# Spreading the inverse roots of two norms over rows: a rounded part and the rest in place of one fp32 operand

## The chip, the cores and the metric

The kernel runs on one core of a Trainium2 chip. The metric is device time in microseconds (us) of one launch, as the median of several runs. TensorE (PE in the profile) does matrix products into PSUM, the accumulator memory (eight banks). VectorE (DVE), ScalarE (ACT) and GpSimd (POOL) work elementwise, and SyncE (SP) issues most of the transfers from DRAM. Every engine has a queue of its own that is worked off in order, and engines wait for one another by semaphores: an instruction that waits holds up all that stands behind it on its engine.

## The reference, cut to what matters

One step of a decoder trunk with two layers over 288 tokens (256 of a prompt and 8 x 4 samples), width 1024. A layer has four branches that read one input projection, gates, an output projection, and a SwiGLU block:

```
xn = rmsnorm(x, norm1_g);  z = xn @ w_in + b_in
o_gla = gla_recurrence(q, k, v, log_a, s0)                    # linear attention, 4 heads of 128
o_a = rmsnorm(o_gla, gla_norm_g) * silu(a_r)                  # norm over each head's 128 features
qd = rope(rmsnorm(d_q per head of 64, q_norm_g))              # 8 query heads
kd = rope(rmsnorm(d_k per head of 64, k_norm_g))              # 2 key heads
o_d = windowed_attention(qd, kd, vd)
x = x + (sum_b sigmoid(xn @ w_gate_b + b_gate_b) * (o_b @ w_branch_b)) @ w_out
x = x + (silu(g) * up) @ w_down,   g, up = rmsnorm(x, norm2_g) @ w_gate_up
```

rmsnorm(v) = v * rsqrt(mean(v*v) + 1e-6) * g. Two of these norms matter here: the one of the queries and keys (over 64 features of a head), and the one of the linear attention's output (over 128).

## The kernel before, in words

Features lie on the 128 partitions and the 288 tokens along the free axis. Each layer's weights stream through a ring of four slots as 158 blocks: 34 of the input projection (blocks 0 to 33), 32 of the gates (34 to 65), 16 of the branches, 8 of the output projection, 44 of the SwiGLU input and 24 of its output. A block of the first two stages holds eight 128x128 weight tiles. The weights and activations of these products are each split in two: a part rounded to fp32r (`w_hi`, `x_hi`) and the rest (`w_lo`, `x_lo`), and a tile costs three matmuls that each go over the 288 columns once (L438 hi x hi, L439 hi x lo, L443 lo x hi), so a block is 24 of them. ScalarE writes `w_hi` of block t+3 while TensorE is at about block t (`split`, L906); the subtraction that gives `w_lo` is GpSimd's in the first two stages, but for a few blocks (L1750), and VectorE's later (L1272). The next load of a slot (L338, on SP) waits for that subtraction. Results of the input projection go to banks 0 and 1 in turn, which ScalarE drains (L911, L917); a block can't start before its bank is drained of the block two before.

All small work of the branches is put between the blocks by the table `STEP`: on TensorE and ScalarE a step with number n runs once block n of the layer is through (a step with a lower number than the current block follows its predecessor at once). VectorE has its small work in a fixed order, with the taps of the convolution in between in runs of a given length (`CONV_RUNS`).

The query and key norm goes like this. ScalarE squares five tiles (four of queries, one of keys). TensorE sums them by head (`qk_sums`, step 14, L483, five fp32 matmuls of 128 rows and 32 columns) into rows of banks 2 and 3. ScalarE makes exp(-0.5 ln(.)) of them (`rstd`, Ln at L925, Exp at L928, one of each for 128 rows and one for 32 rows) and writes `r5`. TensorE spreads each root from its row to the 64 rows of its head (`qk_turned`, step 15, L489): five fp32 matmuls of 32 rows x 128 columns with a 0/1 matrix `of_head`, on row strips 0, 1, 2, 3 and 0 of the array, into banks 2 to 6. VectorE multiplies (L1402, L1404) and goes on with the rotary part (L1408 to L1411); TensorE needs the result at step 25 (`scores0`), and VectorE takes the scores up at L1415.

The linear attention's norm: TensorE sums squares at step 52 (L695, with the sum of another norm, L458, behind it), ScalarE makes Ln of both (L1078, L1079) and Exp of both (L1080 `gla_rs`, L1081), and TensorE spreads `gla_rs` at step 53, after gate block 19 (L704): four fp32 matmuls of 32 rows x 128 columns with the 0/1 matrix `spread`, one for each strip, into banks 2, 3, 6 and 7. VectorE waits for them and multiplies (L1539).

The constants lie in one tile `cst`. Its later part comes by one transfer that ScalarE issues at block 6 of layer 0 (L1175); TensorE first waits for it ahead of `lr_sums` (step 8, L475).

Of the kernel before, what the change touches and what calls it, by code (L numbers as in the profile page):

```python
# [27 lines left out]
P = 128  # L28
TS = DEC_B * DEC_T
# [55 lines left out]
PARAMS = _cols  # L85

CONST_AT, _cols = {}, 0
for _name, _n in (("ones", P), ("eps6", 1), ("eps5", 1), ("heads", TS), ("of_head", P), ("ident", P), ("upper", P), ("band", 2 * P),
                  ("new", 2 * (P + TS)), ("seg", T), ("cos", T), ("sin", T),
                  ("gla", 64), ("gla_s", TS), ("of_b", 4 * DEC_B), ("of_4", 2), ("rep", TS), ("spread", P)):  # L90
    CONST_AT[_name] = _cols
    _cols += _n
CONSTS = _cols

STEP = dict(
    chunk1=44, chunk2=45, chunk3=46, gla_spread=53, n1_sums=0, n1_rstd=0, n1_sums0=3, n1_rstd0=3, c_gate0=12,
    lr_sums=8, c_gate=8, qk_sq=14, qk_sums=14, qk_rstd=3, qk_turned=15, scores0=25, tok_copied=27, scores1=9,  # L100
    exp0=20, exp1=25, probs_turned=21, probs_copied=31, prompt_pv=26, prompt_od=25, smp_scores=27, conv0=35,
    conv1=48, exp_s=33, probs_s_turned=35, probs_s_copied=32, smp_pv=26, smp_od=36, decay_in=24, decay_log=22,
    v_copied=40, decay_exp=35, att_in=41, k_copied=43, gelu=46, chunks=43, smp_old=33, old_out=44, smp_out=47,
# [36 lines left out]
def trunk_program(nc, dram):  # L140
# [3 lines left out]
    with ctx:  # L144
        def sb(name, cols, dt=f32):
            return ctx.enter_context(nc.sbuf_tensor(name, [P, *cols], dt))
# [22 lines left out]
        x = sb("x", [KC, T])  # L169
        x_hi, x_lo = sb("x_hi", [KC, T], f32r), sb("x_lo", [KC, T], f32r)  # L170
        z, gate = zg[:, 0:NZ, :], zg[:, NZ:NZ + 4 * KC, :]
        work = sb("work", [6144])
        kv = sb("kv", [2048])
        prm = sb("prm", [PARAMS])
        cst = sb("cst", [CONSTS])
        w_lr = sb("w_lr", [KC, 32])
        w_a2 = sb("w_a2", [2 * P])
        w_sp = sb("w_sp", [4, P])
# [20 lines left out]
        def c(name, n=None, i=0):  # L199
            at = CONST_AT[name] + i  # L200
            return cst[:, at:at + (n or P)]


        added = work[:, 5760:5760 + T]
        sq = work[:, 0:KC * T].rearrange("p (c t) -> p c t", t=T)
        sq5 = work[:, 0:5 * T].rearrange("p (c t) -> p c t", t=T)
        r5 = work[:, 5 * T:10 * T].rearrange("p (c t) -> p c t", t=T)
        prob = work[:, 0:3072]
        prob_t = work[:, 3072:6144]
        prob0 = prob[:, 0:1024].rearrange("p (h k) -> p h k", k=P)  # L210
# [220 lines left out]
        def _(pe):  # L431
# [28 lines left out]
            def mixers(l, l1):  # L460
# [7 lines left out]
                sum_of(7, sq[:, 0, :], "n1_sums")  # L468
                yield from at("lr_sums")
                pe.wait_ge(E("w_lr_ready"), l1)  # L470
                pe.wait_ge(const_in, 16)
                pe.wait_ge(E("x_scaled"), l1)
                for k in range(KC):
                    part = slice(32 * (k % 4), 32 * (k % 4) + 32)
# [8 lines left out]
                    mm = pe.matmul(ps[r, 2 + k // 4, 0:T], c("heads", TS), sq5[:, k, :], start=True, stop=True)  # L483
                mm.then_inc(E("qk_sums"), 1)
                yield from at("qk_turned")
                pe.wait_ge(E("qk_rstd"), l1)
                for k in range(5):
                    r = slice(TS * (k % 4), TS * (k % 4) + TS)
                    mm = pe.matmul(ps[:, 2 + k, 0:T], c("of_head")[r], r5[r, k // 4, :], start=True, stop=True)  # L489
                mm.then_inc(E("qk_sums"), 1)  # L490
                yield from at("scores0")
                pe.wait_ge(E("qk_done"), l1)
# [205 lines left out]
                pe.wait_ge(E("cv_sq_added"), l1)  # L698
                sum_of(5, added, "cv_var")
                yield from at("gla_spread")  # L700
                pe.wait_ge(E("gla_rstd"), l1)
                for h in range(4):
                    r = slice(TS * h, TS * h + TS)
                    mm = pe.matmul(ps[:, GLA_BANKS[h], 0:T], c("spread")[r], gla_rs[r], start=True, stop=True)  # L704
                mm.then_inc(E("gla_spread"), 1)
                yield from at("smp_update0")
                pe.wait_ge(E("k_own_done"), l1)
# [181 lines left out]
        def _(act):  # L889
# [29 lines left out]
            def logs():  # L919
                act.preload_act_table_set("natural_log_exp_and_others")  # L920

            def rstd(l, out, sums, n, eps, event):

                for o, v in zip(out, sums):
                    ins = act.activation(o, v, ACT.Ln, scale=1.0 / n, bias=c(eps, 1)[0:o.shape[0]])  # L925
                link(ins, l)
                for o in out:
                    ins = act.activation(o, o, ACT.Exp, scale=-0.5)  # L928
                ins.then_inc(E(event), 1)
# [20 lines left out]
            def mixers(l, l1):  # L950
# [11 lines left out]
                    ins = act.activation(z[:, C_G + k, :], z[:, C_G + k, :], ACT.Sigmoid, bias=p("b_in", C_G + k))  # L962
                ins.then_inc(E("c_gate"), 1)
                yield from at("qk_sq")
                act.wait_ge(const_in, 16)
                act.wait_ge(E("lr_sums"), l1)
                act.wait_ge(xl_done, x_part_at(l, XN + KC - 1))
                for t in (D_V - 1, D_V):
# [2 lines left out]
                yield from at("qk_rstd")  # L971
                logs()
                act.wait_ge(E("qk_sums"), 2 * l + 1)
                rstd(l, [r5[:, 0, :], r5[0:TS, 1, :]], [ps[:, 2, 0:T], ps[0:TS, 3, 0:T]], HD, "eps6", "qk_rstd")
                yield from at("tok_copied")
                act.wait_ge(E("tok_turned"), l1)
                act.activation(vt[:, :, :].rearrange("p a n -> p (a n)"), ps[:, 6, 0:2 * P], ACT.Copy)
# [99 lines left out]

                act.activation(gla_rs, ps[:, 2, 0:T], ACT.Ln, scale=1.0 / P, bias=c("eps6", 1))  # L1078
                link(act.activation(rs_m[:, :], ps[:, 5, 0:T], ACT.Ln, scale=1.0 / 512, bias=c("eps5", 1)), l)  # L1079
                act.activation(gla_rs, gla_rs, ACT.Exp, scale=-0.5).then_inc(E("gla_rstd"), 1)  # L1080
                act.activation(rs_m[:, :], rs_m[:, :], ACT.Exp, scale=-0.5).then_inc(E("cv_rstd"), 1)  # L1081
                yield from at("r_silu")
# [81 lines left out]
            for l in range(DEPTH):  # L1164
# [3 lines left out]
                for t in range(NZ):  # L1168
                    if t > C_TILES:
                        drain_z(l, t - 1)  # L1170
                    if l == 0 and 2 <= t <= UNSCALED:
                        wait_block(act, l, Z0 + t - 1)
                        act.activation(z[:, t - 1, :], ps[:, (t - 1) % 2, 0:T], ACT.Copy).then_inc(bank_free[(t - 1) % 2], 1)
                    if l == 0 and t == CONSTS_AT:
                        act.dma_start(cst[:, FIRST_CONSTS:CONSTS], dram["consts"][:, FIRST_CONSTS:CONSTS]).then_inc(const_in, 16)  # L1175
                    split(g0 + t + 3)
                    if t == C_TILES - 1:
                        act.wait_ge(E("x_scaled"), l1)
                        for k in range(KC):
                            xn_part(l, k)  # L1180
                    place[0] = t
                    next(mix, None)
# [73 lines left out]
        def _(dve):  # L1256
# [139 lines left out]

            def mixers(l, l1, conv_steps):

                dve.wait_ge(const_in, 16)
                yield  # L1400
                dve.wait_ge(E("qk_sums"), 2 * l + 2)
                dve.scalar_tensor_tensor(out=z[:, D_Q:D_Q + 4, :], in0=z[:, D_Q:D_Q + 4, :], scalar=p("q_g"), in1=ps[:, 2:6, 0:T],  # L1402
# [131 lines left out]
                link(ins, l)  # L1534
                next(cv)
                next(cv)
                dve.wait_ge(E("gla_spread"), l1)
                for h in range(0, 4, 2):
                    ins = dve.scalar_tensor_tensor(out=g_tmp[:, h:h + 2, :], in0=gla_o[:, h:h + 2, :], scalar=p("gla_g"),  # L1539
# [187 lines left out]
        @block.gpsimd  # L1727
        def _(pool):
            def add_squares(n):

                for k in range(1, KC):
                    pool.wait_ge(sq_done, n * KC + (k + 1))
                    if k >= 2:
                        pool.wait_ge(squares, n * (KC - 1) + (k - 1))
                    pool.tensor_tensor(sq[:, 0, :], sq[:, 0, :], sq[:, k, :], ALU.add).then_inc(squares, 1)  # L1735

            pool.wait_ge(raw0_in, 32)
            pool.wait_ge(x_in[3], 16)
            for i in range(KC - X_SPLIT):
                k = X_SPLIT + i  # L1740
                pool.tensor_scalar(sq[:, k, :], x[:, k, :], p("norm1", k), None, ALU.mult).then_inc(E("x_pool"), 1)
                pool.wait_ge(E("x_pool"), 3 * i + 1)
                pool.tensor_copy(x_hi[:, k, :], sq[:, k, :]).then_inc(E("x_pool"), 1)
                pool.wait_ge(E("x_pool"), 3 * i + 2)
                pool.tensor_tensor(x_lo[:, k, :], sq[:, k, :], x_hi[:, k, :].bitcast(f32), ALU.subtract).then_inc(E("x_pool"), 1)

            def lo_part(g):
                slot = g % RING
                pool.wait_ge(hi_done, g + 1)
                pool.tensor_tensor(w_lo[:, slot, :], raw[:, slot, :], w_hi[:, slot, :].bitcast(f32), ALU.subtract).then_inc(lo_pool, 1)  # L1750

            for l in range(DEPTH):
                l1 = l + 1
                for b in range(LO_SWITCH):
                    if not lo_on_vector(l * BLOCKS + b):
                        lo_part(l * BLOCKS + b)
                    if b == G0:
                        pool.wait_ge(small_in, l1 * 48)
                        pool.wait_ge(const_in, 16)
                        pool.tensor_tensor(w_sp[:, :, :], w_sp[:, :, :], c("upper").unsqueeze(1).to_broadcast([P, 4, P]),  # L1760
                                           ALU.mult).then_inc(E("w_sp_masked"), 1)

                for i in range(1, 4):
                    for d in range(KC):
                        t = i * KC + d
                        wait_drained(pool, l, TB + t)
                        if i >= 2:
                            pool.wait_ge(summed, l * (3 * KC) + (i - 2) * KC + d + 1)
                        pool.tensor_tensor(gate[:, d, :], gate[:, d, :], gate[:, t, :], ALU.add).then_inc(summed, 1)  # L1769
                add_squares(2 * l)  # L1770

                for k in range(HC):
                    pool.wait_ge(silu_done, l * HC + (k + 1))
                    pool.tensor_tensor(gate_s[:, k % 2, :], gate_s[:, k % 2, :], rs[:, :], ALU.mult).then_inc(gate_ready, 1)  # L1774
                if l + 1 < DEPTH:
                    add_squares(2 * l + 1)
# [151 lines left out]
```

## Time and profile before

| | |
|---|---|
| median of 3 runs | 1086.16 us (1086.05 to 1086.22) |
| profiled execution, its own time | 1085.59 us |
| its span in the trace | 1083.8 us |
| TensorE busy | 1079.4 us, 8563 matmul records |
| VectorE busy | 693.0 us |
| ScalarE busy | 592.6 us |
| GpSimd busy | 451.7 us |
| transfers | 181.53 MB, 167 GB/s |

The profiled execution's own time is 1.8 us more than its span, which begins with the first instruction and ends with the last. A matmul's record begins when it starts and ends with a modelled drain, so neighbouring records overlap: what one matmul costs its engine is the distance from its start to the next one's. An fp32 matmul leaves two records, each with a weight load of its own; an fp32r matmul leaves one.

### The profile page before, as it was taken

To read this page: it belongs to the slowest core of one execution; us is meant where nothing else is said; L and a number is where in the kernel's file an instruction comes from. 1 tells how busy PE (TensorE), PEld (TensorE's weight loads), DVE (VectorE), ACT (ScalarE), POOL (GpSimd) and SP (SyncE) were. 2 spreads that over 40 slices of the span, in tenths; PEclk is the share of its full clock that TensorE was granted. 3 is DMA by queue.
4 is the path that set the end of the run, shared out by engine and by line. 5 is a ranking of instruction groups with operands and counts; after the bars stand their busy time and mean duration, and the time that the engine had idled before them with its cause. 6 is when DMAs were issued, how large, how long until landed. Compare 5 with 4: busy or idle time off the path is not lost.

```text
span 1083.8 us, 20512 instructions
## 1 busy us (share of the span) xinstructions
PE 1079.4 (100%) x8563; PEld 1056.1 (97%) x8563; DVE 693.0 (64%) x1010; ACT 592.6 (55%) x900; POOL 451.7 (42%) x251
## 2 busy tenths in 40 slices
PE   9999999999999999999999999999999999999999
PEld 9999989999999999999999998999999999999998
DVE  6698689555775555555549756795367765555543
ACT  7555674777455444444446456657765464444431
POOL 2777655673732111101177866656737221111000
PEclk9999999999999999999999999999999999999999
DMA  9755444455556766555545544434545655555552
GB/s 274 276 172 170 142 148 126 128 149 153 175 168 197 206 205 190 168 164 173 176 152 157 167 156 152 150 118 142 154 151 156 215 171 176 156 169 162 180 170 85
DMA packets 62492, 181.53 MB, mean 167 GB/s; under 512 B 16416, under 2 KB 19232, under 8 KB 61728
## 3 DMA queue, kind: packets, MB, share of 16 engines
q1 hardware_dynamic: 61392, 176.07, 53.1%
q10 hardware_dynamic: 1008, 4.15, 1.1%
q8 instruction: 68, 1.11, 0.4%
q14 instruction: 24, 0.20, 0.1%
HBM read 174.96 MB, written 7.27 MB: 168 GB/s over the span
## 4 chain that ended last, share of the span: by engine, by line
PE 99%; ACT 0%; DVE 0%; issue 0%
PE ps L438 31%; PE ps L443 30%; PE ps L439 30%; PE ps L458 1%; PE ps L754 1%; PE ps L630 0%; PE ps L523 0%; PE ps L748 0%; PE ps L573 0%; PE ps L453 0%; PE ps L651 0%; PE ps L642 0%; PE ps L581 0%; PE ps L489 0%; PE ps L719 0%; PE ps L475 0%
## 5 line engine op out<-in xcount | busy, mean ns | idle before, releaser
L438 PE MATMUL ps<-x_hi,w_hi 128*128 128x288 f32 x1952 | 583.8, 299 | 0.2 <-DVE w_lo L1272 0.2
L439 PE MATMUL ps<-x_lo,w_hi 128*128 128x288 f32 x1952 | 575.8, 295 | 0.0
L443 PE MATMUL ps<-x_hi,w_lo 128*128 128x288 f32 x1952 | 574.0, 294 | 0.0
L906 ACT ACTIVATE w_hi<-raw 128x1024 fp32r<-128x1024 f32 x314 | 325.8, 1051 | 145.4 <-PE ps L443 127.8
L1750 POOL TENSOR_TENSOR w_lo<-raw,w_hi 128x1024 fp32r<-128x1024 f32 x129 | 332.6, 2591 | 161.8 <-ACT w_hi L906 161.5
L438 PEld LDWEIGHTS ps<-x_hi,w_hi 128*128 128x128 f32 x1952 | 365.8, 187 | 8.1 <-issue 6.2
L443 PEld LDWEIGHTS ps<-x_hi,w_lo 128*128 128x128 f32 x1952 | 367.5, 188 | 0.0
L439 PEld LDWEIGHTS ps<-x_lo,w_hi 128*128 128x128 f32 x1952 | 366.5, 188 | 0.6
L1272 DVE TENSOR_TENSOR w_lo<-raw,w_hi 128x1024 fp32r<-128x1024 f32 x185 | 230.0, 1245 | 118.5 <-ACT w_hi L906 118.4
L1774 POOL TENSOR_TENSOR work<-work,rs 128x288 f32<-128x288 f32 x44 | 35.7, 812 | 237.1 <-ACT work L1233 237.1
L443 PE MATMUL ps<-h_hi,w_lo 128*128 128x288 f32 x352 | 104.4, 296 | 0.0
L438 PE MATMUL ps<-h_hi,w_hi 128*128 128x288 f32 x352 | 104.0, 296 | 0.0
L439 PE MATMUL ps<-h_lo,w_hi 128*128 128x288 f32 x352 | 102.6, 292 | 0.0
L1350 DVE SCALAR_TENSOR_TENSOR ps<-hist_p,prm,ps 128x256 f32<-128x256 f32 x240 | 96.7, 481 | 0.3
L1233 ACT ACTIVATE work<-work 128x288 f32<-128x288 f32 x44 | 19.5, 444 | 107.8 <-DVE work L1705 107.8
L1769 POOL TENSOR_TENSOR zg<-zg 128x288 f32<-128x288 f32 x48 | 53.1, 1130 | 49.1 <-DVE zg L1665 48.9
L911 ACT ACTIVATE zg<-ps,prm 128x288 f32<-128x288 f32 x52 | 25.9, 498 | 79.9 <-PE ps L443 79.9
L1735 POOL TENSOR_TENSOR work<-work 128x288 f32<-128x288 f32 x21 | 25.3, 1205 | 101.4 <-ACT work L1140 101.4
L439 PEld LDWEIGHTS ps<-h_lo,w_hi 128*128 128x128 f32 x352 | 67.1, 191 | 0.0
L438 PEld LDWEIGHTS ps<-h_hi,w_hi 128*128 128x128 f32 x352 | 66.1, 188 | 0.0
L443 PEld LDWEIGHTS ps<-h_hi,w_lo 128*128 128x128 f32 x352 | 66.0, 187 | 0.0
L917 ACT ACTIVATE zg<-ps,prm 128x288 f32<-128x288 f32 x64 | 31.7, 496 | 57.4 <-PE ps L443 57.2
(251 smaller groups left out, 1045.7 us busy)
## 6 DMA issues: line engine op xcount, KB each, us to landing
raw<-in_w_up SPq DMA_DIRECT2D x88, 512.0 KB, 4.3
raw<-in_w_z SPq DMA_DIRECT2D x66, 512.0 KB, 3.7
raw<-in_w_gate SPq DMA_DIRECT2D x64, 512.0 KB, 3.6
raw<-in_w_branch SPq DMA_DIRECT2D x32, 512.0 KB, 3.6
raw<-in_w_down SPq DMA_DIRECT2D x32, 512.0 KB, 3.5
raw<-in_w_out SPq DMA_DIRECT2D x16, 512.0 KB, 3.7
raw<-in_w_down SPq DMA_DIRECT2D x16, 384.0 KB, 3.4
kv<-in_state ACTq DMA_DIRECT2D x2, 1024.0 KB, 4.9
```

The source lines that it names most:

```text
L438: pe.matmul(out, wh, rh, start=start, stop=False)
L439: pe.matmul(out, wh, rl, start=False, stop=False)
L443: return pe.matmul(out, w_lo[:, slot, u * UNIT:(u + 1) * UNIT], rh, start=False, stop=stop)
L906: act.activation(w_hi[:, slot, :], raw[:, slot, :], ACT.Copy).then_inc(hi_done, 1)
L911: ins = act.activation(z[:, t, :], ps[:, t % 2, 0:T], ACT.Identity, bias=p("b_in", t))
L917: act.activation(gate[:, t, :], ps[:, t % 2, 0:T], ACT.Identity, bias=p("b_gate", t)).then_inc(bank_free[t % 2], 1)
L1272: dve.tensor_tensor(w_lo[:, slot, :], raw[:, slot, :], w_hi[:, slot, :].bitcast(f32), ALU.subtract)\
L1350: ins = dve.scalar_tensor_tensor(out=acc, in0=src, scalar=w, in1=acc, op0=ALU.mult, op1=ALU.add)
L1735: pool.tensor_tensor(sq[:, 0, :], sq[:, 0, :], sq[:, k, :], ALU.add).then_inc(squares, 1)
L1750: pool.tensor_tensor(w_lo[:, slot, :], raw[:, slot, :], w_hi[:, slot, :].bitcast(f32), ALU.subtract).then_inc(lo_pool, 1)
L1769: pool.tensor_tensor(gate[:, d, :], gate[:, d, :], gate[:, t, :], ALU.add).then_inc(summed, 1)
L1774: pool.tensor_tensor(gate_s[:, k % 2, :], gate_s[:, k % 2, :], rs[:, :], ALU.mult).then_inc(gate_ready, 1)
```

## The change

Both 0/1 matrices go to a tile of their own, `cst_r`, of type fp32r. They come by a second transfer behind the first, into the first columns of the gate tile (unused at that time), and GpSimd copies them from there.

The roots are written twice. ScalarE makes the Exp with fp32r as output type (`rq_hi`, `ra_hi`), waits for it, and then makes the same Exp in fp32 as before. The difference of the two is the rest (`rq_lo`, `ra_lo`): for queries and keys GpSimd makes it, after its subtraction of block 17, with two instructions; for the linear attention VectorE makes it with one. TensorE then spreads the rounded part and adds the rest in the same banks: ten fp32r matmuls for five fp32 ones, and eight for four. The query and key spread moves from step 15 to step 17. Waits on the constants ask for both transfers.

```diff
-    lr_sums=8, c_gate=8, qk_sq=14, qk_sums=14, qk_rstd=3, qk_turned=15, scores0=25, tok_copied=27, scores1=9,
+    lr_sums=8, c_gate=8, qk_sq=14, qk_sums=14, qk_rstd=3, qk_turned=17, scores0=25, tok_copied=27, scores1=9,
...
-        cst = sb("cst", [CONSTS])
+        cst = sb("cst", [PLAIN])
+        cst_r = sb("cst_r", [CONSTS - PLAIN], f32r)
+        work_r = nc.alloc_sbuf_tensor_at("work_r", [P, 6144], f32r, offset=work_at)
...
+        spread_in = gate[:, 0, 0:2 * P]
+        of_head_r, spread_r = cst_r[:, 0:P], cst_r[:, P:2 * P]
...
+        rq_hi, rq_lo = work_r[:, 7 * T:9 * T]..., work_r[:, 0:2 * T]...
+        ra_hi, ra_lo = work_r[:, 5 * T:6 * T], work_r[:, 6 * T:7 * T]
...
-                pe.wait_ge(const_in, 16)
+                pe.wait_ge(const_in, 32)
...
                 yield from at("qk_turned")
-                pe.wait_ge(E("qk_rstd"), l1)
-                for k in range(5):
-                    r = slice(TS * (k % 4), TS * (k % 4) + TS)
-                    mm = pe.matmul(ps[:, 2 + k, 0:T], c("of_head")[r], r5[r, k // 4, :], start=True, stop=True)
+                pe.wait_ge(E("qk_rstd"), 2 * l1)
+                for part in (rq_hi, rq_lo):
+                    for k in range(5):
+                        r = slice(TS * (k % 4), TS * (k % 4) + TS)
+                        mm = pe.matmul(ps[:, 2 + k, 0:T], of_head_r[r], part[r, k // 4, :], start=part is rq_hi, stop=part is rq_lo)
...
                 yield from at("gla_spread")
-                pe.wait_ge(E("gla_rstd"), l1)
-                for h in range(4):
-                    r = slice(TS * h, TS * h + TS)
-                    mm = pe.matmul(ps[:, GLA_BANKS[h], 0:T], c("spread")[r], gla_rs[r], start=True, stop=True)
+                pe.wait_ge(E("gla_rstd"), 2 * l1)
+                for part in (ra_hi, ra_lo):
+                    for h in range(4):
+                        r = slice(TS * h, TS * h + TS)
+                        mm = pe.matmul(ps[:, GLA_BANKS[h], 0:T], spread_r[r], part[r], start=part is ra_hi, stop=part is ra_lo)
...
                 link(ins, l)
+                for h, o in zip(upper, out):
+                    ins = act.activation(h, o, ACT.Exp, scale=-0.5)
+                if upper:
+                    link(ins, l)
                 for o in out:
                     ins = act.activation(o, o, ACT.Exp, scale=-0.5)
                 ins.then_inc(E(event), 1)
...
+                link(act.activation(ra_hi, gla_rs, ACT.Exp, scale=-0.5), l)
                 act.activation(gla_rs, gla_rs, ACT.Exp, scale=-0.5).then_inc(E("gla_rstd"), 1)
...
-                        act.dma_start(cst[:, FIRST_CONSTS:CONSTS], dram["consts"][:, FIRST_CONSTS:CONSTS]).then_inc(const_in, 16)
+                        act.dma_start(cst[:, FIRST_CONSTS:PLAIN], dram["consts"][:, FIRST_CONSTS:PLAIN]).then_inc(const_in, 16)
+                        act.dma_start(spread_in, dram["consts"][:, PLAIN:CONSTS]).then_inc(const_in, 16)
...
                 next(cv)
+                dve.wait_ge(E("gla_rstd"), 2 * l + 1)
+                dve.tensor_tensor(ra_lo, gla_rs, ra_hi.bitcast(f32), ALU.subtract).then_inc(E("gla_rstd"), 1)
                 dve.wait_ge(E("gla_spread"), l1)
...
                     if not lo_on_vector(l * BLOCKS + b):
                         lo_part(l * BLOCKS + b)
+                    if b == 17:
+                        if l == 0:
+                            pool.wait_ge(const_in, 32)
+                            pool.tensor_copy(cst_r[:, :], spread_in)
+                        pool.wait_ge(E("qk_rstd"), 2 * l + 1)
+                        pool.tensor_tensor(rq_lo[:, 0, :], r5[:, 0, :], rq_hi[:, 0, :].bitcast(f32), ALU.subtract)
+                        pool.tensor_tensor(rq_lo[0:TS, 1, :], r5[0:TS, 1, :], rq_hi[0:TS, 1, :].bitcast(f32), ALU.subtract).then_inc(E("qk_rstd"), 1)
```

## Rows read from the trace of the kernel before

**Rows 1.** The page's head and its part 1: busy us (share) x instructions.
```profile
span 1083.8 us, 20512 instructions
...
PE 1079.4 (100%) x8563; PEld 1056.1 (97%) x8563; DVE 693.0 (64%) x1010; ACT 592.6 (55%) x900; POOL 451.7 (42%) x251
```

**Rows 2.** Waits of TensorE: who waited for whom, us in total, times, longest.
```profile
PE ps L754 <- DVE zg_r L1589: 1.2, 1, 1.2
PE ps L438 <- DVE w_lo L1272: 0.2, 1, 0.2
```

**Rows 3.** Timeline, TensorE, layer 0, block 15's end: start us, us, instruction.
```profile
62.54 0.29 PE L443 MATMUL ps<-x_hi,w_lo 128*128 128x288 f32 x1
62.77 1.23 PE L489 MATMUL ps<-work,cst 32*128 32x288 f32 x10
63.93 0.40 PE L438 MATMUL ps<-x_hi,w_hi 128*128 128x288 f32 x1
```

**Rows 4.** Timeline in two narrower windows of the same stretch.
```profile
62.77 0.53 PE L489 MATMUL ps<-work,cst 32*128 32x288 f32 x4
...
63.36 0.64 PE L489 MATMUL ps<-work,cst 32*128 32x288 f32 x2
```

**Rows 5.** Timeline, TensorE, layer 0, behind gate block 19.
```profile
212.02 0.77 PE L704 MATMUL ps<-work,cst 32*128 32x288 f32 x8
212.72 0.40 PE L438 MATMUL ps<-x_hi,w_hi 128*128 128x288 f32 x1
```

**Rows 6.** Timeline, matmuls and weight loads (PEld) inside a block, layer 0.
```profile
65.36 0.29 PE L439 MATMUL ps<-x_lo,w_hi 128*128 128x288 f32 x1
...
66.16 0.29 PE L439 MATMUL ps<-x_lo,w_hi 128*128 128x288 f32 x1
...
65.50 0.19 PEld L438 LDWEIGHTS ps<-x_hi,w_hi 128*128 128x128 f32 x1
```

**Rows 7.** Timeline, ScalarE, layer 0, the query and key roots and what follows.
```profile
59.48 0.87 ACT L925 ACTIVATE work<-ps,cst 128x288 f32<-128x288 f32 x2 [0.23 <-PE ps L483]
60.39 0.78 ACT L928 ACTIVATE work<-work 128x288 f32<-128x288 f32 x2
61.07 0.48 ACT L911 ACTIVATE zg<-ps,prm 128x288 f32<-128x288 f32 x1
```

**Rows 8.** Timeline, ScalarE, layer 0, roots of the linear attention's norm.
```profile
209.92 0.45 ACT L1080 ACTIVATE work<-work 128x288 f32<-128x288 f32 x1
210.27 0.43 ACT L1081 ACTIVATE rs_m<-rs_m 128x288 f32<-128x288 f32 x1
```

**Rows 9.** Timeline, GpSimd: blocks 18, 19 (layer 0), 20 to 24 (layer 1).
```profile
62.57 5.68 POOL L1750 TENSOR_TENSOR w_lo<-raw,w_hi 128x1024 fp32r<-128x1024 f32 x2 [2.85 <-ACT w_hi L906]
...
605.34 15.65 POOL L1750 TENSOR_TENSOR w_lo<-raw,w_hi 128x1024 fp32r<-128x1024 f32 x5 [1.64 <-ACT w_hi L906]
```

**Rows 10.** Timeline, VectorE, both layers, where it takes the products up.
```profile
78.45 1.41 DVE L1402 SCALAR_TENSOR_TENSOR zg<-zg,prm,ps 128x1152 f32<-128x1152 f32 x1
...
601.05 1.41 DVE L1402 SCALAR_TENSOR_TENSOR zg<-zg,prm,ps 128x1152 f32<-128x1152 f32 x1
...
634.15 1.22 DVE L1415 SCALAR_TENSOR_TENSOR work<-ps,cst 128x1024 f32<-128x1024 f32 x1 [17.79 <-PE ps L501]
...
212.86 1.54 DVE L1539 SCALAR_TENSOR_TENSOR work<-zg,prm,ps 128x576 f32<-128x576 f32 x2 [8.42 <-PE ps L704]
```

**Rows 11.** Groups by form: busy us, mean ns of one, idle before.
```profile
L1774 POOL TENSOR_TENSOR work<-work,rs 128x288 f32<-128x288 f32 x44 | 35.7, 812 | 237.1 <-ACT work L1233 237.1
...
L1714 DVE TENSOR_TENSOR h_lo<-work,h_hi 128x288 fp32r<-128x288 f32 x44 | 19.9, 452 | 0.0
```

**Rows 12.** The constants: transfer (KB, us to landing), its issue, the first user.
```profile
cst<-in_consts ACTq DMA_DIRECT2D x1, 1073.0 KB, 7.2
...
26.09 0.33 ACTq L1175 DMA_DIRECT2D cst<-in_consts  x1
...
L475 PE MATMUL ps<-work,w_lr x32: 406/406/430, 37.8 to 574.9; 128*32 128x288 f32 x32
```

More of the change, by code:

```diff
@@ L87 @@
 CONST_AT, _cols = {}, 0
-for _name, _n in (("ones", P), ("eps6", 1), ("eps5", 1), ("heads", TS), ("of_head", P), ("ident", P), ("upper", P), ("band", 2 * P),
+for _name, _n in (("ones", P), ("eps6", 1), ("eps5", 1), ("heads", TS), ("ident", P), ("upper", P), ("band", 2 * P),
                   ("new", 2 * (P + TS)), ("seg", T), ("cos", T), ("sin", T),
-                  ("gla", 64), ("gla_s", TS), ("of_b", 4 * DEC_B), ("of_4", 2), ("rep", TS), ("spread", P)):
+                  ("gla", 64), ("gla_s", TS), ("of_b", 4 * DEC_B), ("of_4", 2), ("rep", TS), ("of_head", P), ("spread", P)):
     CONST_AT[_name] = _cols
@@ L93 @@
 CONSTS = _cols
+PLAIN = CONST_AT["of_head"]
 STEP = dict(
     chunk1=44, chunk2=45, chunk3=46, gla_spread=53, n1_sums=0, n1_rstd=0, n1_sums0=3, n1_rstd0=3, c_gate0=12,
-    lr_sums=8, c_gate=8, qk_sq=14, qk_sums=14, qk_rstd=3, qk_turned=15, scores0=25, tok_copied=27, scores1=9,
+    lr_sums=8, c_gate=8, qk_sq=14, qk_sums=14, qk_rstd=3, qk_turned=17, scores0=25, tok_copied=27, scores1=9,
     exp0=20, exp1=25, probs_turned=21, probs_copied=31, prompt_pv=26, prompt_od=25, smp_scores=27, conv0=35,
@@ L171, in trunk_program @@
         z, gate = zg[:, 0:NZ, :], zg[:, NZ:NZ + 4 * KC, :]
+        work_at = -(-nc.sbuf_base // 32) * 32
         work = sb("work", [6144])
@@ L207, in trunk_program @@
         r5 = work[:, 5 * T:10 * T].rearrange("p (c t) -> p c t", t=T)
+        rq_hi, rq_lo = work_r[:, 7 * T:9 * T].rearrange("p (c t) -> p c t", t=T), work_r[:, 0:2 * T].rearrange("p (c t) -> p c t", t=T)
+        ra_hi, ra_lo = work_r[:, 5 * T:6 * T], work_r[:, 6 * T:7 * T]
         prob = work[:, 0:3072]
@@ L920, in logs, with rstd @@
                 act.preload_act_table_set("natural_log_exp_and_others")
-            def rstd(l, out, sums, n, eps, event):
+            def rstd(l, out, sums, n, eps, event, upper=()):
                 for o, v in zip(out, sums):
@@ L964, in mixers @@
                 yield from at("qk_sq")
-                act.wait_ge(const_in, 16)
+                act.wait_ge(const_in, 32)
                 act.wait_ge(E("lr_sums"), l1)
@@ L973, in mixers @@
                 act.wait_ge(E("qk_sums"), 2 * l + 1)
-                rstd(l, [r5[:, 0, :], r5[0:TS, 1, :]], [ps[:, 2, 0:T], ps[0:TS, 3, 0:T]], HD, "eps6", "qk_rstd")
+                rstd(l, [r5[:, 0, :], r5[0:TS, 1, :]], [ps[:, 2, 0:T], ps[0:TS, 3, 0:T]], HD, "eps6", "qk_rstd",
+                     [rq_hi[:, 0, :], rq_hi[0:TS, 1, :]])
                 yield from at("tok_copied")
@@ L1397, in mixers @@
             def mixers(l, l1, conv_steps):
-                dve.wait_ge(const_in, 16)
+                dve.wait_ge(const_in, 32)
                 yield
@@ L1756, in _ @@
                         lo_part(l * BLOCKS + b)
+                    if b == 17:
[5 more added lines that the diff above has]
+                        pool.tensor_tensor(rq_lo[0:TS, 1, :], r5[0:TS, 1, :], rq_hi[0:TS, 1, :].bitcast(f32), ALU.subtract).then_inc(E("qk_rstd"), 1)
                     if b == G0:
                         pool.wait_ge(small_in, l1 * 48)
-                        pool.wait_ge(const_in, 16)
+                        pool.wait_ge(const_in, 32)
                         pool.tensor_tensor(w_sp[:, :, :], w_sp[:, :, :], c("upper").unsqueeze(1).to_broadcast([P, 4, P]),
```

## The prediction

> **What bounds the kernel now.** I read the page's head first: TensorE is busy for 1079.4 of 1083.8 us, every other engine for 64% or less [rows 1]. Busy time alone would not settle it, since its records overlap, so next the waits of TensorE: 1.4 us in all, none near the change [rows 2]. So TensorE's queue sets the end, every instruction taken from it or put into it counts in full, and every other engine counts only where it makes that queue wait. Then the timeline around the two spreads, where distances from start to start are read.
>
> **What a spread costs now.** The query and key spread starts at 62.77 and the next block at 63.93: 1.16 us [rows 3]. Its ten records are two for each fp32 matmul. Four of them start together at 62.77, and the last two, those of the fifth matmul, which shares strip 0 with the first, start from 63.36 on [rows 4]: the four strips run side by side, and strip 0 with four records is the longest. I read 1.16 as a start S plus four records of strip 0, and the other spread, two records on each strip, as S plus two: 212.72 - 212.02 = 0.70 us [rows 5]. The difference of two records is 0.46, so a record costs 0.23 (a little more by the gap that the 288 columns need twice) and S is 0.24; with 0.24 for a record S is 0.2. The latter is taken.
>
> **What it costs after.** An fp32r matmul over 288 columns costs (66.16 - 65.36) / 6 = 0.133 us inside a block [rows 6]. That is for 128 rows; the trace has none on 32. If strips still run side by side, strip 0 gets four of them for queries and keys (first and fifth matmul, both parts): 0.2 + 4 x 0.133 = 0.73, a gain of 0.43. For the linear attention each strip gets two: 0.2 + 2 x 0.133 = 0.47, a gain of 0.23. Together 0.66 for a layer, 1.33 for two. The number of matmul records stays (ten for ten, eight for eight), so no gain can come from there.
>
> Bounds. Below: if S vanished too, at both places of both layers, 4 x 0.2 = 0.8 more, a gain of 2.1. Above: if fp32r matmuls of different strips ran one after another, ten cost 0.2 + 1.33 = 1.53 (a loss of 0.37) and eight 0.2 + 1.06 = 1.26 (a loss of 0.56), 1.9 us lost over two layers. I take the gain of 1.33: row strips did run side by side, and nothing in the rows ties that to the type.
>
> The Trainium skill has a rule against this: "TensorE: Matmul & The Clock Gate", section "Part 3: Packing small matmuls", lets a weight load run beside matmuls only if it goes to another row group. Strip 0 would then pay each load before its matmul. The rows of a full block speak against it: a load starts with the matmul before it (65.50 beside 65.50) and lasts 0.19, and matmuls are still 0.133 apart [rows 6]. It stays a rival below.
>
> **Waits that the change adds, by the place where TensorE would feel them.**
>
> ScalarE, queries and keys: two more Exps. The two of now start at 60.39, last 0.78, and the drain of block 14 starts at 61.07 and lasts 0.48 [rows 7]. Two more and a semaphore between make it 0.82 later: end 62.37. Block 16 needs that bank, and it now starts right behind block 15, since the spread no longer stands between: 62.54 + 0.133 = 62.67 [rows 3]. 0.3 us are left, and the same in layer 1 by the same distances. Cost 0; if Exps or the semaphore take 0.5 longer, 0.2 a layer.
>
> GpSimd: two subtractions of 288 columns (0.81 each [rows 11]; up to some 1.2 beside a busy VectorE) from about 62.0, so the rest is there by 63.6 to 64.4. The spread now stands behind block 17: two more blocks of 24 x 0.133 = 3.2 after 62.67, so 69.1. Cover 4.7 us. In layer 0 the copy of the constants (256 columns) lies in the time in which GpSimd waited 2.85 us for ScalarE before block 18 [rows 9]. Queued behind: the subtractions of blocks 18 and 19, which ran from 62.57 to 68.25 [rows 9]; they start about 1.6 to 2 us later. Block 18 needs its own at 69.1 + 0.73 = 69.8, and it would be done by 67.6. Cost 0; the loads on SP that wait for a subtraction start later by as much and have blocks of room. In layer 1 GpSimd is the fullest, five subtractions in 15.65 us for a supply of one in 3.2 [rows 9]; its delay of under 2 us finds it idle for 1.64 before block 20, so again nothing.
>
> VectorE: in layer 0 it reached the product at 78.45, after the new time as well. In layer 1 it took it up at 601.05 [rows 10]; the spread there will end at about 606.3, so VectorE now waits some 5.3 us. Behind it are the rotary part and a few taps, and then it was idle for 17.79 us before the scores at 634.15 [rows 10]: that idle time swallows it, and TensorE gets the rotary result ahead of step 25. Cost 0; without that cover it would be 5.3 us once.
>
> Linear attention: the Exp of now starts at 209.92 and lasts 0.45 [rows 8]. One more ahead of it: the fp32 root at 210.86. VectorE's subtraction takes 0.45 [rows 11] and VectorE stands idle there, for 8.42 us before 212.86 [rows 10], so the rest is there at about 211.4. TensorE comes at 212.02 [rows 5]: 0.6 us are left. The Exp and the drains behind on ScalarE are 0.45 later, without reaching their users. Cost 0; half a microsecond of delay more and it would begin to cost.
>
> Constants: one transfer of 1073 KB was issued at 26.09 and landed 7.2 later, at 33.3; the first user stands at 37.8 [rows 12]. The same bytes in two transfers, the second issued 0.33 later: about 34. Cost 0.
>
> **The sum.** Span 1083.8 - 1.33 = 1082.5. The profiled execution's own time is 1.8 above its span, 1085.59, so 1084.26 for it; the median of the runs is 1086.16, 0.57 above, and gives 1084.8.
>
> **The rivals.**
>
> *Strips in turn.* The fp32r matmuls of different strips run one after another. For it: no row shows fp32r on a strip. Against: four fp32 records start within the first moment [rows 4]. 1.9 us lost: 1088.0, slower than before. It decides as soon as the pitch of the ten exceeds (1.16 - 0.2) / 10 = 0.096 us.
>
> *Weight loads exposed.* By the skill's rule above each matmul pays its load. With the load's 0.19 and 0.12 of streaming [rows 6], four on strip 0 cost 0.2 + 1.24 = 1.44 (0.28 lost) and two 0.82 (0.12 lost): 1087.0 over two layers; with strips in turn as well, ten and eight times 0.31, 8 us lost: 1094. Against: rows 6 and the fp32 records, whose 0.24 have no room for a load of 0.19.
>
> *No single pass on strips, or the gain is waited away.* If an fp32r matmul on 32 rows costs what a record of fp32 does (0.24), ten take what ten took: 1086.2. The same comes out if the margin of 0.3 at block 16 and of 0.6 at the linear attention are both overrun by 0.3 us.
>
> *More than counted.* The start S and the slow first matmul of the next block (its record lasts 0.40 where those inside a block last 0.29 [rows 3, 6]) shrink as well once no fp32 matmul stands there: at most 0.3 for each of four places, 1083.6.
>
> **Chances.** Forecast 0.63, with its own range 1084.2 to 1085.5. Strips in turn 0.12, loads exposed 0.07, gain gone 0.12, more than counted 0.06. The range goes from 1083.9 to 1088.2: it holds the forecast, the strips in turn and most of the rest. 0.2% of this kernel is 2.2 us, about what a measurement can tell from no change; the forecast's 1.33 is 0.12%. Faster by more (below 1084.0): most of the last rival, 0.07. Slower by more (above 1088.3): part of the strips in turn and of the exposed loads, 0.10. Within it 0.83.
>
> **What would show it.** Right: 0.73 and 0.47 from the first record of the spreads to the next block's, no new wait of TensorE, the spread of the queries behind block 17, and VectorE waiting some 5 us for it in layer 1 but 12 or so before the scores. Wrong: records of the spreads that start 0.1 or more apart (strips in turn), a wait of the first matmul of block 16 for ScalarE, a wait of the linear attention's spread for VectorE, or of a block from 18 to 24 for GpSimd.

## The result, and the profile after

The changed kernel takes 1090.08 us (median of 5 runs, 1088.76 to 1091.36) where the kernel before takes 1086.17 on the same chip: a ratio of 1.0037, 95% interval 1.0027 to 1.0048. It is slower, by 3.9 us. The forecast was 1084.8 with a range from 1083.9 to 1088.2, and the chance given to a time above 1088.3 was 0.10.

The profiled execution is the fastest of the five (1088.76, with a mean granted clock of 1.000). Its page, head and part 1, to be read beside [rows 1]:

```profile
span 1087.0 us, 20526 instructions
...
PE 1078.5 (99%) x8563; PEld 1055.7 (97%) x8563; DVE 700.5 (64%) x1012; ACT 594.2 (55%) x906; POOL 456.0 (42%) x256
```

TensorE is 0.9 us less busy in a span that is 3.2 us longer: the work got cheaper and something else came in. The waits of TensorE say what (who waited for whom, us in total, times, longest), against [rows 2]:

```profile
PE ps L504 <- DVE zg L1429: 3.4, 1, 3.4
PE ps L765 <- DVE zg_r L1609: 1.2, 1, 1.2
PE ps L447 <- POOL x_lo L1765: 0.5, 1, 0.5
PE ps L447 <- DVE w_lo L1290: 0.4, 1, 0.4
```

L504 is the first instruction of `scores0`, and L1429 the last of the rotary part. It is one wait, in layer 0. The spreads themselves did what was forecast. Timeline of TensorE, the query and key spread in layer 0 and the linear attention's in layer 1 (start us, us), for [rows 3, 5]:

```profile
69.79 0.79 PE L499 MATMUL ps<-work_r,cst_r 32*128 32x288 f32 x10
70.51 0.40 PE L447 MATMUL ps<-x_hi,w_hi 128*128 128x288 f32 x1
...
751.70 0.53 PE L715 MATMUL ps<-work_r,cst_r 32*128 32x288 f32 x8
752.16 0.40 PE L447 MATMUL ps<-x_hi,w_hi 128*128 128x288 f32 x1
```

From the start of a spread to the next block it is 0.72 us (1.16 before) and 0.46 (0.70 before). Why VectorE is late stands in the timelines of VectorE and GpSimd in layer 0, for [rows 9, 10]:

```profile
62.32 1.19 DVE L1345 TENSOR_REDUCE zg<-work 128x32 f32<-128x992 f32 x1
63.54 8.84 DVE L1343 TENSOR_TENSOR work<-hist_s,prm 128x992 f32<-128x992 f32 x1
72.42 1.19 DVE L1345 TENSOR_REDUCE zg<-work 128x32 f32<-128x992 f32 x1
73.64 2.06 DVE L1343 TENSOR_TENSOR work<-hist_s,prm 128x992 f32<-128x992 f32 x1
84.84 1.41 DVE L1420 SCALAR_TENSOR_TENSOR zg<-zg,prm,ps 128x1152 f32<-128x1152 f32 x1
...
62.68 0.81 POOL L1782 TENSOR_TENSOR work_r<-work,work_r 128x288 fp32r<-128x288 f32 x1 [1.99 <-ACT work L943]
63.45 0.80 POOL L1783 TENSOR_TENSOR work_r<-work,work_r 32x288 fp32r<-32x288 f32 x1
64.22 10.43 POOL L1770 TENSOR_TENSOR w_lo<-raw,w_hi 128x1024 fp32r<-128x1024 f32 x4
75.54 2.42 POOL L1770 TENSOR_TENSOR w_lo<-raw,w_hi 128x1024 fp32r<-128x1024 f32 x1 [0.89 <-ACT w_hi L917]
```

L1343 multiplies taps with samples for the convolution, with both operands in SBUF. It takes 1.19 us alone and 2.06 where it meets one of GpSimd's subtractions halfway; here one of the four takes 8.84, while GpSimd goes from one subtraction to the next. Such a row joins instructions that lie close together, and a short gap is hidden inside the four: three subtractions of 2.36 from 64.22 on end at 71.3, and ScalarE has the rounded weights for the fourth ready only then (first row; 70.30 + 1.05 = 71.35). GpSimd is busy for 0.21 of the next 0.30 us (second row: stretch, length, busy, count, granted clock, share and rate of transfers), and in this gap VectorE gets in: 63.54 + 8.84 = 72.38, less the 1.19 of the work itself, is 71.19.

```profile
70.30 1.05 ACT L917 ACTIVATE w_hi<-raw 128x1024 fp32r<-128x1024 f32 x1
...
71.30:71.60 0.30, 0.21 (x2) 1.00 0.96 396
```

VectorE takes the product of the queries up at 84.84 where it did at 78.45 [rows 10], and TensorE stands still between these two instructions:

```profile
96.08 0.29 PE L452 MATMUL ps<-x_hi,w_lo 128*128 128x288 f32 x1
99.82 0.44 PE L504 MATMUL ps<-cst,zg 128*128 128x128 f32 x2 [3.45 <-DVE zg L1429]
```

The four other runs took 1.3 to 2.6 us more than this one, with a mean granted clock of 0.997 or 0.998 in place of 1.000; no trace of them is kept, but the trace of qk_only below shows a lowered clock at this place.

### The profile page after: what moved, and what is told of

Its sections match the earlier page's. It is cut to its first block, busy times and chain, and to the rows that moved or that the text cites. A ratio compares the mean times of both kernels' runs of the same rounds, so it can differ in the third digit from the quotient of the medians.

```text
span 1087.0 us, 20526 instructions
## 1 busy us (share of the span) xinstructions
PE 1078.5 (99%) x8563; PEld 1055.7 (97%) x8563; DVE 700.5 (64%) x1012; ACT 594.2 (55%) x906; POOL 456.0 (42%) x256
## 4 chain that ended last, share of the span: by engine, by line
PE 93%; DVE 4%; ACT 1%; DMA 1%; POOL 0%; issue 0%; SPq 0%; DVEq 0%; ACTq 0%; POOLq 0%
PE ps L447 30%; PE ps L452 29%; PE ps L448 29%; DVE work L1343 1%; PE ps L467 1%; DMA x<-in_x 1%; DVE zg L1345 0%; PE ps L640 0%; DVE hist_p L1329 0%; PE ps L533 0%; DVE zg L1428 0%; DVE zg L1429 0%; DVE work L1427 0%; DVE ps L1368 0%; PE ps L759 0%; PE ps L583 0%
```

## The experiments

All are compared with the kernel before on the same chip. The `dummy` kernels and gap32 are the kernel before with work for GpSimd added; the others are the changed kernel with one part of it altered or left as before.

**gla_only: the linear attention's part alone.** Query and key code as before.

```diff
-    qk_turned=17
+    qk_turned=15
-                for part in (rq_hi, rq_lo): ... of_head_r[r], part[r, k // 4, :]
+                mm = pe.matmul(ps[:, 2 + k, 0:T], c("of_head")[r], r5[r, k // 4, :], start=True, stop=True)
```

> Only the linear attention's spread is changed (rounded part on ScalarE, rest on VectorE, eight fp32r matmuls); queries and keys as before at step 15. My theory: the loss sits in the query and key part alone, where GpSimd works without a break and VectorE's product L1343 of layer 0 is held off (8.84 us where it took 3.24). Then this kernel is faster than before by the spread's 0.23 us in each layer: 1085.7 of 1086.2, no wait of TensorE at scores0, and no lowered clock. Rival (the linear attention's chain ScalarE, VectorE, TensorE costs as well): slower than before.

Measured: 1085.71 us, ratio 0.9996 (0.9987 to 1.0005), no wait at `scores0`. The direction is the expected one, but 0.46 us is inside the interval. The loss of 3.9 us isn't here.

**qk_only: the query and key part alone.** The linear attention's code as before.

> Only the query and key spread is changed, the linear attention as before. My theory: TensorE waits 3 to 4 us for VectorE at scores0 of layer 0, L1343 is held for 8 us or more, and the time is the changed kernel's plus about 0.46: 1089 to 1092. Rival (loss is shared by both parts): clearly under the changed kernel's time.

Measured: 1090.92 us, ratio 1.0042 (1.0029 to 1.0056), a wait of 3.4 us at `scores0`. So the loss is in this part. In its timeline VectorE met GpSimd one step later than in the changed kernel and was held for 9.89 us:

```profile
63.52 1.19 DVE L1341 TENSOR_TENSOR work<-hist_s,prm 128x992 f32<-128x992 f32 x1
65.97 9.89 DVE L1341 TENSOR_TENSOR work<-hist_s,prm 128x992 f32<-128x992 f32 x1
...
63.54 1.84 POOL L1779 TENSOR_TENSOR work_r<-work,work_r 32x288 fp32r<-32x288 f32 x1
65.34 9.45 POOL L1766 TENSOR_TENSOR w_lo<-raw,w_hi 128x1024 fp32r<-128x1024 f32 x4
```

Four subtractions in 9.45 us are 2.36 each: none of them was slowed, VectorE got nothing in between. Its profiled execution (1091.08 us) also shows the second part of the loss. Stretches of layer 0 (us; busy and count by engine; then the granted clock, the share and rate of the transfers):

```profile
96.20:99.90 3.70, 0.26 (x2) 0.03 (x1) 3.70 (x2) 1.45 (x2) 3.70 (x2) 1.00 0.49 145
99.90:102.00 2.10, 2.09 (x18) 1.86 (x20) 1.53 (x4) 0.00 (x0) 2.10 (x1) 0.66 0.50 201
102.00:104.00 2.00, 2.00 (x14) 1.37 (x12) 1.38 (x2) 0.00 (x0) 0.06 (x1) 0.51 0.44 84
104.00:106.00 2.00, 2.00 (x16) 1.89 (x15) 1.93 (x6) 0.00 (x0) 0.00 (x0) 1.00 0.47 186
```

TensorE stands still for 3.7 us at a clock of 1.00; right behind, the granted clock is 0.66 and then 0.51 on the mean, which is 1.2 GHz in place of 2.4 for about all of the second of these stretches, and then full again. As an estimate, with work at half the clock taking twice its time, the two stretches give away 2.10 x 0.34 + 2.00 x 0.49 = 1.7 us. With the 0.46 that the linear attention's old spread costs, that is the 2.3 us between this execution and the profiled one of the changed kernel, but for 0.17. In the profiled execution of the changed kernel the clock stayed at 1.00 behind a wait of the same length: the wait was in every trace with a held product and `scores0` at step 25, the lowered clock not in this one.

**no_rest: GpSimd's two subtractions left out.** TensorE spreads the rounded part twice in place of the rounded part and the rest, so the kernel leaves the rest out; GpSimd's copy of the constants moves to block 14 (not printed here), and all else of the change stays.

```diff
-                for part in (rq_hi, rq_lo):
+                for n, part in enumerate((rq_hi, rq_hi)):
-                        pool.tensor_tensor(rq_lo[:, 0, :], ...)
-                        pool.tensor_tensor(rq_lo[0:TS, 1, :], ...)
```

> GpSimd's two subtractions are left out: TensorE spreads the rounded part of the query and key roots twice (so the result of that norm is left wrong), all else of the change stays, ScalarE's second Exps among it; the copy of the constants stands at block 14. If GpSimd's subtractions hold VectorE off (my theory): L1343 goes back to some 3 us, no wait at scores0, 1084.8 to 1085.5. If the later start of block 18's rounded weights on ScalarE (the two more Exps) already fills GpSimd's queue without a gap, or the step 17 makes VectorE late: the wait of 3 us stays and the time is over 1088.

Measured: 1084.93 us, ratio 0.9989 (0.9980 to 0.9998), no wait at `scores0`. ScalarE's two more Exps and step 17 are all still there. So it is the work on GpSimd behind block 17: the subtractions, or the copy, which has moved too. The run wide below keeps the copy in its place and loses nothing, so it is the subtractions.

**dummy: GpSimd's load without the change.** The kernel before with

```diff
+                    if b == 17:
+                        pool.wait_ge(E("qk_rstd"), l1)
+                        for i in range(4):
+                            pool.tensor_tensor(gate[:, 1 + i, :], x[:, i, :], x[:, i + 1, :], ALU.subtract)
```

> The kernel before, with nothing of the change but four subtractions of 288 columns on GpSimd behind its block 17, from tiles nobody writes at that time into unused columns; they move its block 18 from 62.6 to about 64.4, as in the changed kernel. My theory: L1343 is held off through several of GpSimd's subtractions again, VectorE is some 5 us late, TensorE waits 2 to 4 us at scores0 of layer 0: 1088.5 to 1091. Rival (the spread in fp32r, step 17 or ScalarE's Exps are needed for the loss): 1086.2 as before.

Measured: 1086.24 us, ratio 1.0002 (0.9993 to 1.0011). My theory fell: GpSimd works without a gap from 61.4 to 81.7 and VectorE isn't held.

```profile
62.91 1.23 DVE L1325 TENSOR_TENSOR work<-hist_s,prm 128x992 f32<-128x992 f32 x1
65.40 1.23 DVE L1325 TENSOR_TENSOR work<-hist_s,prm 128x992 f32<-128x992 f32 x1
67.88 2.06 DVE L1325 TENSOR_TENSOR work<-hist_s,prm 128x992 f32<-128x992 f32 x1
...
61.42 4.16 POOL L1760 TENSOR_TENSOR zg<-x 128x288 f32<-128x288 f32 x4 [1.53 <-ACT work L928]
65.53 16.14 POOL L1750 TENSOR_TENSOR w_lo<-raw,w_hi 128x1024 fp32r<-128x1024 f32 x6
```

Here the six take 2.69 each, some of them slowed by VectorE: the two take turns. A full queue is not enough. What the added work lacked was the change's second subtraction, on 32 rows only. The next two runs turn that one property both ways.

**wide: the changed kernel, the second subtraction on 128 rows.**

```diff
-                        pool.tensor_tensor(rq_lo[0:TS, 1, :], r5[0:TS, 1, :], rq_hi[0:TS, 1, :].bitcast(f32), ALU.subtract)
+                        pool.tensor_tensor(rq_lo[:, 1, :], r5[:, 1, :], rq_hi[:, 1, :].bitcast(f32), ALU.subtract)
```

ScalarE's rounded Exp for it goes over 128 rows as well (not printed here).

> The changed kernel with its second GpSimd subtraction over all 128 rows in place of 32 (and ScalarE's rounded Exp for it likewise; the further rows are read by nobody). Same count, columns and place. Theory A (since the last run): GpSimd gets out of step with itself by the instruction on 32 rows, so that its following subtractions pass to one another without letting VectorE in; with 128 rows VectorE gets in at the next boundary, L1343 takes 3.3 us or less, TensorE waits for nobody at scores0: 1084.9. Theory B (a full queue of GpSimd is enough, whatever the rows): L1343 stays at 8 us or more, the wait of 3.4 us stays, 1088.7 to 1091.5.

Measured: 1084.95 us, ratio 0.9989 (0.9980 to 0.9998), no wait at `scores0`.

```profile
63.50 1.76 DVE L1343 TENSOR_TENSOR work<-hist_s,prm 128x992 f32<-128x992 f32 x1
66.52 2.06 DVE L1343 TENSOR_TENSOR work<-hist_s,prm 128x992 f32<-128x992 f32 x1
...
63.39 0.81 POOL L1783 TENSOR_TENSOR work_r<-work,work_r 128x288 fp32r<-128x288 f32 x1
64.17 17.08 POOL L1770 TENSOR_TENSOR w_lo<-raw,w_hi 128x1024 fp32r<-128x1024 f32 x6
```

The two GpSimd instructions take as long as in the changed kernel (0.81 each, against 0.81 and 0.80), start within 0.06 us of where they did, and VectorE's product starts 0.04 us from where it did; 8.84 has become 1.76.

**dummy32: the kernel before with the last of the four on 32 rows.**

```diff
+                            r = slice(0, TS if i == 3 else P)
+                            pool.tensor_tensor(gate[r, 1 + i, :], x[r, i, :], x[r, i + 1, :], ALU.subtract)
```

> The four added subtractions of the run dummy in the kernel before, the last of them on 32 rows in place of 128, all else the same. Theory A: VectorE's next product with two operands in SBUF that meets GpSimd's queue is held for 7 to 10 us, TensorE waits 1 to 4 us at scores0 of layer 0: 1087.5 to 1091. Theory B: as dummy, 1086.2.

Measured: 1092.61 us, ratio 1.0059 (1.0047 to 1.0072), more than expected. Nothing of the change is in it, and VectorE is late by this:

```profile
65.76 10.68 DVE L1325 TENSOR_TENSOR work<-hist_s,prm 128x992 f32<-128x992 f32 x1
...
61.77 4.15 POOL L1761 TENSOR_TENSOR zg<-x 128x288 f32<-128x288 f32 x4 [1.52 <-ACT work L928]
65.89 9.49 POOL L1750 TENSOR_TENSOR w_lo<-raw,w_hi 128x1024 fp32r<-128x1024 f32 x4
75.88 2.81 POOL L1750 TENSOR_TENSOR w_lo<-raw,w_hi 128x1024 fp32r<-128x1024 f32 x1 [0.50 <-ACT w_hi L906]
```

VectorE is let in only when GpSimd has run out: the four end at 75.38, and the 10.68 us end at 76.44, 1.06 later, where the product alone takes 1.19. It isn't the moment at which the two engines meet: in dummy, too, the product starts 0.13 us ahead of GpSimd's first block subtraction (65.40 and 65.53 there, 65.76 and 65.89 here), and takes 1.23.

TensorE waits for 3.5 us at `scores0`, as in the changed kernel. The time is longer than there because the clock fell for longer: in the profiled execution (1093.33 us) it is 0.50 from 100 to 106 us, and by the same estimate as for qk_only 3.4 us are given away.

**vec_rest: the rest made by VectorE.** In layer 0 its two subtractions stand behind the second pair of sample taps (first run of `CONV_RUNS` 2 and then 7 in place of 8 and 1).

> The changed kernel with the query and key rest made by VectorE (two subtractions, in layer 0 behind the second pair of sample taps) and none by GpSimd; the copy of the constants at block 14. Both theories: no wait at scores0, L1343 at 3 us or less, VectorE 0.9 us more work ahead of its product in layer 0, under the 2.4 us that are to spare at scores0: 1084.9. If the fp32r spreads themselves disturb VectorE: over 1087.

Measured: 1085.22 us, ratio 0.9991 (0.9982 to 1.0000). No wait at `scores0`, as expected; it can't be told apart from wide, and its interval ends at no change.

**scores26: the changed kernel with `scores0` one block later.**

> The changed kernel with step scores0 at 26 in place of 25, so that one more block of 3.2 us stands ahead of TensorE's wait. If the time is lost by this wait and the lowered clock behind it: the wait shrinks to about 0.2 us, the clock stays full, and the time is 3.2 us or more under the changed kernel's fastest run, about 1085.3, if what follows (exps, transposed scores) has a block to spare. L1343 stays at 8 us or more under every theory.

Measured: 1085.61 us, ratio 0.9994 (0.9985 to 1.0003). L1343 is still held for 8.85 us, and the wait is 0.3 us:

```profile
PE ps L504 <- DVE zg L1429: 0.3, 1, 0.3
```

So the held instruction costs little by itself: the median is 0.7 us above that of wide, and 0.3 of it is this wait. The loss is TensorE's wait for what stands behind the held product, and the clock after it.

**dummy64: the last of the four on 64 rows.**

> As dummy32, but the last of the four added GpSimd subtractions is on 64 rows. If any instruction on fewer rows than 128 puts GpSimd out of step (theory A, in its general form): VectorE's product is held for 7 us or more and the time is 1089 to 1093, as dummy32. If it is special to 32 rows: 1086.2, as dummy.

Measured: 1091.69 us, ratio 1.0053 (1.0039 to 1.0067), L1325 at 65.65 held for 10.67 us. So it is nothing special to 32 rows.

**dummy_first: the narrow one first, three of 128 rows behind it.**

> As dummy32, but the first of the four is the one on 32 rows and three on 128 rows follow it without a gap. Theory A says that the state lasts until GpSimd runs out of ready instructions, not only for the next one: VectorE is held until about 75 us in layer 0, L1325 at 62.9 already (over 10 us), time 1089 to 1095. If only the instruction right behind a narrow one matters: L1325 is held once for 3 to 4 us, 1086 to 1087.

Measured: 1092.95 us, ratio 1.0062 (1.0048 to 1.0075).

```profile
63.22 1.24 DVE L1325 TENSOR_TENSOR work<-hist_s,prm 128x992 f32<-128x992 f32 x1
65.71 10.67 DVE L1325 TENSOR_TENSOR work<-hist_s,prm 128x992 f32<-128x992 f32 x1
...
61.72 4.16 POOL L1761 TENSOR_TENSOR zg<-x 32x288 f32<-32x288 f32 x4 [1.52 <-ACT work L928]
65.84 9.48 POOL L1750 TENSOR_TENSOR w_lo<-raw,w_hi 128x1024 fp32r<-128x1024 f32 x4
```

The state outlasts three full instructions. One detail was expected wrongly: the product at 63.22 got through in 1.24 us, and only the next was held. Why that one was let in, these rows don't show.

**gap32: one subtraction on 32 rows, and then nothing to do.** The kernel before with a single one behind block 17 that waits for nobody.

> The kernel before with one single GpSimd subtraction on 32 rows behind its block 17, which waits for nobody, so that GpSimd stands idle for some 2 us after it. Theory A: the gap brings it back into step, L1325 at 62.75 takes 3.2 us as before, 1086.2. If a narrow instruction has its effect whatever follows: L1325 at 8 us or more, 1088.5 or more.

Measured: 1086.13 us, ratio 1.0001 (0.9992 to 1.0010). GpSimd stands idle for 2.11 us behind it, and VectorE's product takes 2.67:

```profile
63.80 2.67 DVE L1325 TENSOR_TENSOR work<-hist_s,prm 128x992 f32<-128x992 f32 x1
...
60.14 0.80 POOL L1758 TENSOR_TENSOR zg<-x 32x288 f32<-32x288 f32 x1
63.05 5.69 POOL L1750 TENSOR_TENSOR w_lo<-raw,w_hi 128x1024 fp32r<-128x1024 f32 x2 [2.11 <-ACT w_hi L906]
```

**one_rest: both subtractions as one of 128 rows and 576 columns.**

> A version meant to beat both: the kernel of run wide with GpSimd's two subtractions over 128 rows made one of 576 columns. No narrow instruction of GpSimd is left. 1084.9 as wide, or up to 0.2 us from it; VectorE's L1343 at 3 us or less, no wait at scores0. If a longer single instruction of GpSimd holds VectorE more than two short ones: L1343 at 63.5 takes 0.8 us longer, still without a wait of TensorE.

Measured: 1085.27 us, ratio 0.9991 (0.9982 to 1.0000), L1343 at 1.64 and 2.05 us. It is far under the changed kernel's 1090.08, but its interval against the kernel before ends at no change; wide and it can't be told apart.

## Why the prediction was wrong

**What bounds the kernel: right.** TensorE's queue sets the end, and other engines count where it waits.

**The spreads: right.** Forecast 0.73 and 0.47 us, measured 0.72 and 0.46. fp32r matmuls on different strips run side by side as the fp32 ones do, so the rival of strips in turn and the one of exposed weight loads fell (in turn, ten would have taken 1.53; at 0.31 us for each, four on strip 0 could not fit into 0.72). The 0.12 us of streaming in that rival stands in no row of [rows 6], which show 0.133 from start to start; with either figure it is too long. The forecast of 1084.8 is what the change gives once GpSimd's instruction is wide: 1084.95 in wide.

**ScalarE, the linear attention and the constants: right.** The drain of block 14 ended 0.3 us ahead of the start of block 16 in the timeline (62.97 and 63.30), the linear attention's rest had 0.7 us to spare, and no wait on either stands among TensorE's waits.

**VectorE in layer 1: right.** 5.3 us of wait and some 12 of idle time were forecast:

```profile
610.13 1.41 DVE L1420 SCALAR_TENSOR_TENSOR zg<-zg,prm,ps 128x1152 f32<-128x1152 f32 x1 [5.26 <-PE ps L499]
...
637.46 1.23 DVE L1433 SCALAR_TENSOR_TENSOR work<-ps,cst 128x1024 f32<-128x1024 f32 x1 [12.03 <-PE ps L511]
```

That GpSimd's queue did no harm there was luck, since the prediction didn't ask: its four subtractions behind the narrow one ended at 613.34, and VectorE's first product with two operands in SBUF came at 613.85.

**GpSimd in layer 0: wrong, and this is the step that failed.** The prediction put its two subtractions at 0.81 us each, "up to some 1.2 beside a busy VectorE", looked at what stands behind them on GpSimd and at who waits for that, found cover for all, and set "Cost 0". It counted how VectorE slows GpSimd and not how GpSimd slows VectorE, and it said of VectorE in layer 0 that "it reached the product at 78.45, after the new time as well", as if 78.45 could not move. It moved to 84.84. No row of the prediction shows the 1.2 either; the two took 0.81 and 0.80, and in qk_only the second took 1.84.

What it missed stood in the trace of the kernel before, in layer 0: a product of VectorE that met GpSimd already took 3.24 us, and the rotary part's last instruction (L1411) ended only 2.80 us before `scores0` (L494) started.

```profile
62.75 3.24 DVE L1325 TENSOR_TENSOR work<-hist_s,prm 128x992 f32<-128x992 f32 x1
...
89.49 3.74 DVE L1411 TENSOR_TENSOR zg<-zg,work 128x1440 f32<-128x1440 f32 x1
...
96.03 0.38 PE L494 MATMUL ps<-cst,zg 128*128 128x128 f32 x2
```

In the changed kernel that instruction ends at 99.76, 6.53 later, and TensorE would have come to `scores0` 0.18 later than before: 6.53 - 2.80 - 0.18 = 3.55 us, where by its own starts TensorE lost 3.6. I looked this margin up for layer 1 alone.

What the runs put in its place: a GpSimd instruction on fewer than 128 rows (32 and 64 tried), followed by others without a gap, lets the followers pass to one another without letting VectorE's instruction with two SBUF operands in. Shown are both directions (wide, dummy32), that it outlasts full instructions (dummy_first), and that a narrow one with 2.11 us of idle time behind it does nothing (gap32). Layer 1 has the same narrow instruction and no loss, since VectorE waits for the spread there while GpSimd works its queue off.

The Trainium skill, "SBUF — State Buffer", section "Who interferes with whom", has VectorE and GpSimd share one pair of ports under an exclusive lock held for a whole instruction. The rows with full instructions agree: in dummy VectorE's product waits at most one GpSimd instruction out, 2.06 us in place of 1.23. The kernel before agrees too: the 3.24 us are what was left of GpSimd's subtraction (62.57 to about 64.9) and the 1.19 of the product. If the two take turns under such a lock, a product never waits for more than one; 8.84 to 10.68 us differ from that, and the measurement decides. The Trainium skill, "GPSIMD Engine Reference", section "Specifications", gives GpSimd eight cores with 16 partitions each. That cores without rows in the narrow instruction run ahead, so that some core is always in the next instruction at the boundary, would explain the held products. It does not say why the product at 63.22 in dummy_first got through, and no run here looks at single cores: it is not shown, and why a narrow instruction does this stays open.

**The size.** The span of the profiled execution grew by 3.2 us. By starts in the timelines: block 26 of layer 0 began at 98.52 before and at 102.36 after, 3.84 later, made of about 3.6 for the wait, 0.6 that were there from the start, and 0.44 less for the spread; behind it the other three spreads give 0.9 back, and 0.3 are unexplained. Of the 0.6, 0.5 are the wait for `x_lo` in the table of waits above, and 0.1 a longer one for `w_lo`. The traces of dummy64 and dummy32 show both too, without anything of the change at the start, so I don't put them down to the change. From the profiled executions to the medians: the median run of the changed kernel takes 1.3 us more than its profiled one, at a mean clock of 0.998, and the median of the kernel before 0.6 more than its own: 3.2 + 1.3 - 0.6 = 3.9.

**Its rivals.** None was about VectorE being held, and a wait at `scores0` wasn't among the signs of being wrong. The chance of 0.10 for a time above the range rested on the array, and so did the numbers that made the range.

## What to carry to other kernels

When work is given to GpSimd, ask which instructions of VectorE with two operands in SBUF run beside it, and how late each may be: the price lies on the other engine, and on TensorE if that one's result has a fixed step. Keep GpSimd's elementwise instructions at 128 rows when its queue is full, even if most rows are thrown away: 128 rows took the 0.81 us that 32 took, and it was worth 5.1 us here. A wait of TensorE of some 3.5 us can cost more than itself: in four of the five runs of the changed kernel the mean granted clock was below 1.000, and they took 1.3 to 2.6 us more than the fifth.

## What the runs showed of the hardware

- A GpSimd subtraction of 288 columns takes 0.80 us on 32 rows and 0.81 on 128.
- A VectorE product of 992 columns, both operands in SBUF: 1.19 us alone, 1.23 to 3.24 where it meets GpSimd instructions on 128 rows, 8.84 to 10.68 when these stand in a row behind a narrow one.
- fp32r matmuls of 32 rows on four strips: (0.72 - 0.46) / 2 = 0.13 us for each further one on the same strip, and four strips at once, since ten of them took 0.72 us.
- In the profiled execution of qk_only the granted clock fell from 1.00 to 0.51 behind 3.7 us in which TensorE stood still, and in dummy32 it was at 0.50 for 6 us around the end of such a wait. With the same wait and a full clock the changed kernel took 1088.76; its runs with a mean clock of 0.997 or 0.998 took 1090.02 to 1091.36.
